# A ring of two raw weight buffers instead of three, the third place left unused

## What is computed

```
first_block, per layer (x: 256 x 1024):
    h = x @ w_in                                  # 1024 x 9216
    o_a = retention(rq, rk, rv, rg)               # 4 heads, chunks of 64
    o_b = chunk_attention(cq, ck, cv, rel_bias)   # 8 heads
    o_c = diff_attention(dq, dk, dv, lam)         # 4 head pairs
    merged = g0 * (o_a @ w_branch_a) + g1 * (o_b @ w_branch_b) + g2 * (o_c @ w_branch_c)
    x = layer_norm(ALPHA * x + merged @ w_out)
    x = layer_norm(ALPHA * x + (silu(x @ gate) * (x @ up)) @ w_ffn_out)    # hidden 2816
second_block, per layer:
    x = layer_norm(ALPHA * x + 0.5 * swiglu(x, ffn1))                      # hidden 2816
    proj = x @ w_in_2
    y = concat(short_conv, gmlp_spatial, nsa_attention)
    x = layer_norm(ALPHA * x + y @ w_out_2)
    x = layer_norm(ALPHA * x + 0.5 * swiglu(x, ffn2))
```

## Time and profile before

| | |
|---|---|
| median of 3 runs | 1985.08 us (1984.97 to 1985.42) |
| profiled execution | 1985.54 us, of which the span is 1983.7 us |
| TensorE matmul busy | 1971.5 us (99%) |
| TensorE weight load busy | 1800.7 us (91%) |
| VectorE busy | 1246.3 us (63%) |
| ScalarE busy | 911.0 us (46%) |
| GpSimd busy | 99.7 us (5%) |
| mean DMA rate | 182 GB/s |
| granted TensorE clock | full in all 40 slices |

### The profile page before, as it was taken

How to read it: one execution, slowest core, us unless ns; L and a number is a source line. 1 busy time by engine, 2 the same in 40 slices (tenths; PEclk the granted TensorE clock), 3 DMA queues, 4 the chain that set the end, 5 groups by cost and what they waited for, 6 DMA issues and landing times.

```text
span 1983.7 us, 31862 instructions
## 1 busy us (share of the span) xinstructions
PE 1971.5 (99%) x13856; PEld 1800.7 (91%) x13856; DVE 1246.3 (63%) x1772; ACT 911.0 (46%) x1221; POOL 99.7 (5%) x84
## 2 busy tenths in 40 slices
PE   8999999999999999999999999999999999999998
PEld 7888999999888999999999989899999998989997
DVE  6566666555656766655565567665566556776555
ACT  4445544444445545444444445544444444555442
POOL 0000001000100000100110020010010002001000
PEclk9999999999999999999999999999999999999999
DMA  8544566666554456696666656468666665646663
GB/s 291 174 144 143 178 205 197 198 208 191 172 168 149 140 179 195 196 261 186 175 211 191 188 154 170 111 196 258 191 170 210 187 186 150 177 120 195 185 188 106
DMA packets 421445, 361.85 MB, mean 182 GB/s; under 512 B 29424, under 2 KB 361528, under 8 KB 421304
## 3 DMA queue, kind: packets, MB, share of 16 engines
q1 hardware_dynamic: 421160, 359.74, 60.0%
q10 hardware_dynamic: 144, 0.07, 0.0%
HBM read 358.72 MB, written 1.05 MB: 181 GB/s over the span
## 4 chain that ended last, share of the span: by engine, by line
PE 99%; DVE 0%; DMA 0%; DVEq 0%; ACT 0%; issue 0%
PE ps L217 23%; PE ps L219 23%; PE ps L218 23%; PE ps L224 8%; PE ps L226 8%; PE ps L225 8%; PE ps L1521 3%; PE ps L1632 1%; PE ps L1666 1%; PE ps L1637 0%; PE ps L1704 0%; PE ps L1655 0%; DMA xs<-in_x 0%; PE ps L1772 0%; PE ps L1788 0%; PE ps L1681 0%
## 5 line engine op out<-in xcount | busy, mean ns | idle before, releaser
L2040 DVE TENSOR_TENSOR hl<-raw,hl 128x1024 fp32r<-128x1024 f32 (+2 forms) x535 | 722.5, 1384 | 381.3 <-ACT hl L1816 380.7
L217 PE MATMUL ps<-xt,hl 128*128 128x256 f32 (+1 forms) x2672 | 754.2, 282 | 0.0
L218 PE MATMUL ps<-xt,hl 128*128 128x256 f32 (+1 forms) x2672 | 746.1, 279 | 0.0
L219 PE MATMUL ps<-xt,hl 128*128 128x256 f32 (+1 forms) x2672 | 745.8, 279 | 0.0
L1816 ACT ACTIVATE hl<-raw 128x2048 fp32r<-128x2048 f32 (+1 forms) x338 | 613.9, 1825 | 222.9 <-PE ps L226 162.5
L217 PEld LDWEIGHTS ps<-xt,hl 128*128 128x128 f32 (+1 forms) x2672 | 500.9, 187 | 5.5 <-issue 2.3
L218 PEld LDWEIGHTS ps<-xt,hl 128*128 128x128 f32 (+1 forms) x2672 | 501.0, 188 | 3.2
L219 PEld LDWEIGHTS ps<-xt,hl 128*128 128x128 f32 (+1 forms) x2672 | 500.8, 187 | 0.2
L224 PE MATMUL ps<-hl,o 128*128 128x512 f32 x656 | 261.6, 399 | 0.0
L226 PE MATMUL ps<-hl,o 128*128 128x512 f32 x656 | 259.0, 395 | 0.0
L225 PE MATMUL ps<-hl,o 128*128 128x512 f32 x656 | 258.8, 394 | 0.0
(11 more groups left out here) (197 smaller groups left out, 1576.2 us busy)
## 6 DMA issues: line engine op xcount, KB each, us to landing
raw<-in_w_in SPq DMA_DIRECT2D x83, 1024.0 KB, 5.1
raw<-in_w_ffn_in SPq DMA_DIRECT2D x88, 512.0 KB, 5.2
raw<-in_ffn_gate SPq DMA_DIRECT2D x88, 512.0 KB, 4.0
raw<-in_ffn_up SPq DMA_DIRECT2D x88, 512.0 KB, 5.3
raw<-in_ffn_down SPq DMA_DIRECT2D x44, 1024.0 KB, 5.2
raw<-in_w_ffn_out SPq DMA_DIRECT2D x22, 1024.0 KB, 5.1
raw<-in_w_out SPq DMA_DIRECT2D x24, 512.0 KB, 4.9
raw<-in_w_branch_a SPq DMA_DIRECT2D x8, 1024.0 KB, 5.1
```

Of the source, the lines that this page charges most:

```text
L217: e.matmul(out, l[0], r[0], start=start, stop=False)
L218: e.matmul(out, l[0], r[1], start=False, stop=False)
L219: return e.matmul(out, l[1], r[0], start=False, stop=stop)
L2040: e.tensor_tensor(lo[:, c], m["raw"][:, k % NRAW, 0:n][:, c], hi[:, c].bitcast(F), ALU.subtract).then_inc(s.low.up(("low", k), *([("low", ...
```

## The change

`NRAW`, the number of raw slots in use, goes from 3 to 2. The tile `raw` keeps its size of three places, so that no other tile moves in memory; the third place is not used.

```
-NRAW = 3
+NRAW = 2
 NHL = 3
...
-            "raw": sb("raw", [128, NRAW, UNIT]), "hl": sb("hl", [128, NHL, 2, UNIT], R),
+            "raw": sb("raw", [128, 3, UNIT]), "hl": sb("hl", [128, NHL, 2, UNIT], R),
```

## The result

The changed kernel takes 2029.91 us (median of four runs, 2027.3 to 2038.2), the kernel before 1985.1 us beside it: a ratio of 1.0233, 95% interval 1.0221 to 1.0245. That is 44.8 us more, against 19.5 forecast, and outside the range. The sign, the four places and the order in which they come were right; the size was not.

The account below looks back on a forecast made before the run. TensorE bounds the kernel, so the change costs exactly its new waiting: 3.6 + 10 + 4.6 + 1.3 = 19.5 us on 1985.54 gives 2005.0, 2004.6 as a median. Range 1996 to 2018, or 1990 to 2026 with part of the rivals.

Parts of the forecast that it names:

- What bounds it: Whole kernel: TensorE is busy nearly all of the span, with only two waits, 5.1 us for input and 0.4 for weights.
- The turn of 9.4 to 9.9 against 11.2 us: Steady FFNs: one slot's load, high and low parts fit the 11.2 us a two-slot ring has, 1.3 to 1.8 spare.
- the turn does not fit: Rival, 13 in 100: FFN landings grow to about 7.3 us, a turn exceeds 11.2 us, giving 2020 to 2035 us.
- Term 1: Two norms between mixer and FFN in block one (309, 802 us): late low part delays norm statistics and transposes, 3.6 us.
- Term 2: FFNs where SP also issues parameters (833 to 890, 1325 to 1385): loads around the burst come late, 10 us in all.
- The norm rows in SP's order: A norm's four parameter rows ahead of a load in SP's queue: counted only within Term 2's 1 to 2 us lateness allowance.
- Term 3: Second block's projections before attention (1207, 1698 us): four-DMA units land late, 2.3 us at each, 4.6 in all.
- Term 4: First 40 us: an already awaited load goes out later and delays work behind it, 1.3 us, between 0 and 4.
- The steady stretches: Steady FFN flow, 198 units: two slots keep up, so the change costs nothing there while the cover stands.
- the cover of 6.9 us: FFNs: finished units in the hl ring hide 6.9 us of lateness of one unit before TensorE must wait.
- The crowded stretches thin out: Rival, 22 in 100: fewer loads in flight queue less around the burst, Term 2 falls away, 1994.6 or 1990 us.
- The signs: Profile after: TensorE waits some 15 us for low parts, transposes 3 to 4, ScalarE over 50 for DMAs; steady FFNs unchanged.

Follow-up runs that it names:

- e1: The kernel before with its three raw slots, every load waiting for the low part of the unit two back instead of three: 2029.55 us.
- e9: The changed kernel with parameter DMAs issued one behind each load and GpSimd's low parts beside a norm waiting for VectorE's second L2104: 2002.88 us.
- e2: The kernel before, only the loads of units 48 and 129, ahead of the two norms, waiting two units back: 1999.02 us.
- e4: e2 with the low parts beside the norms made by VectorE instead of GpSimd: 2003.84 us.
- e5: The kernel before with the low parts beside the norms made by VectorE instead of GpSimd, no load gated later: 1999.91 us.
- e8: The changed kernel with GpSimd's low parts beside a norm waiting until VectorE's second L2104 is done: 2020.38 us.
- e11: The changed kernel with only the norms' row DMAs spread, one behind each load, instead of in a burst: 2023.79 us.
- e10: The kernel before, only the loads of units 200 and 281, in the second block's projections, waiting two units back: 1994.74 us.
- e3: The kernel before, every load waiting two units back except units 48 and 129, which wait three back: 2016.11 us.

## Why the prediction was right in place and wrong in size

- **What bounds it: right.** TensorE had no slack, so every us of new waiting came out at the end, and more than that.
- **The price of a wait: wrong, the first step that failed.** The prediction said that the change costs exactly the time by which TensorE is made to wait anew. In the profile of after 33.0 us of new waits came with 19.5 us of longer busy time, at most 16.6 of them by the half clock behind the waits; in that of e1 it was 27.3 and 13.4. In e9, where waits are few, TensorE's busy time was only 6.4 us above before.
- **The amount of waiting: too small, the second step that failed.** The terms held 19.5 us of waits, the profile of after has 33.0. The largest parts are the norms (9.3 for 3.6) and the norm rows in front of the FFNs (6.1 for nothing), below.
- **The turn of 9.4 to 9.9 against 11.2 us: right.** The 100 us rows are the same before and after, and the rival "the turn does not fit" named a time near the measured one, 2020 to 2035, by a mechanism that didn't occur: it wanted 7.3 us from a slot's release to the last landing, and it was 5.1 behind an issue some 0.4 us later, so 5.5. That its time is near is luck.
- **Term 1, 3.6 us: its path right, its size wrong.** The forecast moved VectorE's queue by the right 1.9 us and then said that there is nothing else in the way. GpSimd's low part, which the change doesn't move, stood at 311.77, 0.25 us before the old end of L2104; a norm that slips by 1.9 us must lie beside it. The waits were 9.3 us; alone (e2) it cost 13.8 with the clock, and without the collision 3.9 (e4 against e5). The 2.1 us for the second layer, for which the prediction shows no row, were 1.51 us of waiting in e4 and 1.46 in e8.
- **Term 2, 10 us: the waits right** (3.87 + 1.08 + 2.69 + 0.80 and 1.00 = 9.4 us), at the matmul that was named. Its clock was not in the term, and the first wait was longer than expected (3.87 for 2.1 to 3.1).
- **The norm rows in SP's order, costed at nothing for the FFNs: wrong.** I had used them only as lateness of term 2. They stand between loads at the beginning of each FFN and cost 6.1 us with what follows (e11).
- **Term 3, 4.6 us: one place right (2.38 for 2.3 us), the other 3.77.** Alone they cost 9.7 (e10), more than the waits. The working names 0.5 us that the queue ahead gives up and then leaves them out of 2.9 - 0.6; in e10 the two low halves slipped by the whole 2.8 us (1205.93 and 1208.36), so leaving them out was right, without a reason given. It did not price the clock and took the second layer for a copy of the first, where the last landing came 8.0 us behind the gate and not 6.5.
- **Term 4, 1.3 us: 2.0 us**, at the place named.
- **The steady stretches at nothing: right**, although the cover of 6.9 us was 5.0 at the unit that was tested.
- **"The crowded stretches thin out": wrong.** The load of the burst goes out behind the later gate and lands later, as the case against it said.
- **The signs.** TensorE waited 22.1 us for low parts where 15 were named, and 9.3 for the norm where 3 to 4 were; ScalarE's waits for data came to 233 us where "over 50" was named, and the steady stretches kept their time.

By the sum: of 33.0 us of waits the terms held 19.5, with 5.7 missing for the norms, 1.6 for the projections, 0.7 for the start and 6.1 for the unlisted norm rows, 0.6 too much for the bursts. The longer busy time, 19.5 us in that profile and mostly the clock, had no term at all and is the largest miss.

## What to carry to other kernels

A ring's depth can't be judged by one turn in the steady state. Look at the joints where a late step stands in front of other work in an in-order queue, and at every burst of small DMAs between two loads; and when a step of VectorE slips, look at what GpSimd does in the stretch into which it slips. Where TensorE sets the time, price each new wait of 2 us or more with the half clock that may follow it: up to 1.7 us for a stretch of 3.41 us and 3.4 us for one of 6.83. Here, with two slots, spreading the small DMAs and making GpSimd's work wait for the norm gave back 27 of 45 us.

## What the runs showed of the hardware

**Half clock behind short waits.** In after, eight waits or pairs of waits of 1.95 to 3.87 us came with 3.41 or 6.83 us at half clock. The wait of 5.1 us with which the program starts, that of 2.0 us at 41.06 and those of 1.13 us and less did not. It is not the length of the wait alone: at the first projections a wait of 2.49 us in e1 and one of 2.70 in e9 had no half clock, one of 2.53 us in e3 had. In e3 itself a wait of the same 2.53 us at 863.74 had none, and in e8 neither had one of 2.62 us at 1372.19. TensorE's row and the granted clock behind it in e1, and then in e3:

```profile
1233.89 0.39 PE L217 MATMUL ps<-xt,hl 128*128 128x256 f32 x1 [2.49 <-DVE hl L2041]
...
1234.00:1238.00 4.00, 4.00 (x58) 3.87 (x60) 3.22 (x4) 0.92 (x2) 3.51 (x3) 1.00 0.92 178
```

```profile
1219.61 0.38 PE L218 MATMUL ps<-xt,hl 128*128 128x256 f32 x1 [2.53 <-DVE hl L2042]
...
1222.00:1226.00 4.00, 4.00 (x58) 3.69 (x55) 1.02 (x1) 0.00 (x0) 1.61 (x2) 0.74 1.30 235
```

The granted clock behind the first is 1.00, behind the second 0.74. What decides between them stays open. It may be part of why after, e1 and e3 vary by 4.6 to 10.9 us from run to run and the kernel before by 0.5 to 1.0 us. It isn't all of it: of the 11.9 us between the spans in the profiles of after and e1, which have the same gate, 6.1 are busy time and 5.7 are waits.

**VectorE beside GpSimd.** The scalar-tensor-tensor with both tensor inputs in SBUF (L2104) went from 1.41 to 5.01 us for two. The one ahead of it (L2099), which reads one of them from PSUM, is not slowed by the same GpSimd instruction. The kernel before shows it at each of its seven norms with one; at the first:

```profile
314.22 2.42 POOL L1993 TENSOR_TENSOR hl<-raw,hl 128x1024 fp32r<-128x1024 f32 x1
315.72 0.75 DVE L2099 SCALAR_TENSOR_TENSOR xs<-ps,small,et 128x512 f32<-128x512 f32 x1
```

It lies beside GpSimd for its whole length and takes 0.75 us; the one at 309.76, with GpSimd idle, takes 0.74. It matters which one is first: before, an L2104 that had started at 311.27 kept its 0.74 us although GpSimd began at 311.77.
